# Hybrid encoder layer on eight cores: the last stage gates on unnormalised tiles, takes its reciprocal roots by Newton steps on GpSimd and transposes p first

## The reference, cut to what matters

```python
def rmsnorm(x, g):
    r = lax.rsqrt(jnp.mean(xf * xf, axis=-1, keepdims=True) + EPS)
    return (xf * r).astype(x.dtype) * g
...
        x = x + mix @ w_out[i]
        h = rmsnorm(x, g_ffn[i])
        x = x + hier_moe(h, ...)          # top-1 group, top-2 of its 8 experts
        gate = jax.nn.sigmoid(rmsnorm(x, g_ple[i]) @ w_ple_gate[i])
        x = x + (p[i] @ w_ple_proj[i]) * gate
    return rmsnorm(x, g_final)
```

## Time and profile before

| what | us |
|---|---|
| median of 3 runs | 1676.73 |
| lowest, highest of them | 1671.33, 1725.31 |
| time of the profiled execution | 1667.38 |
| its span, on core 6, the slowest | 1666.1 |
| spans of the 8 cores | 1635.5 to 1666.1 |

### The profile page before, as it was taken

The page is one execution under the profiler, slowest core; times in us unless marked ns, Lnnn a source line. Parts: engine busy times, 40 slices in busy tenths (PEclk is TensorE's granted clock), DMA queues, the critical chain, the costliest instruction groups (busy, mean ns, idle before and its releaser), DMA issues.

```text
span 1666.1 us, 22293 instructions; the slowest of 8 cores (1635.5 to 1666.1 us)
## 1 busy us (share of the span) xinstructions
PE 1117.0 (67%) x7796; PEld 704.6 (42%) x7835; DVE 572.1 (34%) x1050; ACT 474.3 (28%) x756; POOL 259.4 (16%) x285
## 2 busy tenths in 40 slices
PE   0126999999999885664645185766767657731784
PEld 0123444556656443433434174545645446520332
DVE  4452221445545434444414321111212112110476
ACT  1231111434323554322213021111212112212764
POOL 2010330000001002000000121223322223237300
PEclk9999999978768797877766597878878878875887
DMA  4749699999999999999998489789898797799813
GB/s 80 177 134 127 84 113 111 110 111 109 112 110 109 110 122 128 146 183 130 150 129 131 151 256 270 201 229 242 230 287 211 211 271 192 184 168 203 174 77 127
DMA packets 79267, 266.50 MB, mean 160 GB/s; under 512 B 17033, under 2 KB 23209, under 8 KB 69936
## 3 DMA queue, kind: packets, MB, share of 16 engines
q0 software_dynamic: 53680, 153.65, 64.7%
q1 hardware_dynamic: 25472, 111.36, 20.7%
HBM read 350.94 MB, written 113.79 MB: 279 GB/s over the span
## 4 chain that ended last, share of the span: by engine, by line
PE 45%; DMA 29%; DVE 9%; issue 9%; ACT 5%; POOL 2%; DVEq 0%; SPq 0%; another core or an unknown queue 0%; ACTq 0%; POOLq 0%
DMA arena<-h2d,arena 17%; PE ps L460 10%; PE ps L561 6%; DMA arena<-xl 6%; PE ps L1164 5%; PE ps L543 4%; DMA ohd<-arena 4%; PE ps L1145 4%; PE ps L531 4%; PE ps L1361 3%; PE ps L601 2%; PE ps L877 1%; PE ps L1124 1%; POOL arena L1312 1%; PE ps L435 1%
## 5 line engine op out<-in xcount | busy, mean ns | idle before, releaser
L547 ACT ACTIVATE arena<-ps 128x1024 bf16<-128x1024 f32 (+4 forms) x152 | 137.3, 916 | 192.6 <-PE ps L543 192.3
L1145 PE MATMUL ps<-arena 128*128 128x192 bf16 x2048 | 176.2, 247 | 1.1 <-ACT arena L1131 1.1
L1145 PEld LDWEIGHTS ps<-arena 128*128 128x128 bf16 x2048 | 171.5, 98 | 8.1 <-issue 1.3
L1164 PE MATMUL ps<-arena 128*96 128x512 bf16 x512 | 153.9, 459 | 15.2 <-DVE arena L1152 11.7
L460 PE MATMUL ps<-arena 128*128 128x512 bf16 (+1 forms) x744 | 161.2, 377 | 1.0 <-issue 0.2
L1124 PE MATMUL ps<-arena 96*128 96x96 bf16 x512 | 40.7, 245 | 159.8 <-DMA arena<-h2d,arena 159.8
L877 PE MATMUL ps<-arena 128*128 128x512 bf16 x242 | 74.9, 471 | 87.1 <-DVE arena L858 42.4
L1177 POOL DMA_INDIRECT y<-arena x64 | 60.6, 946 | 368.6 <-ACT arena L1169 289.7
L561 PE MATMUL ps<-arena 128*65 128x128 bf16 (+5 forms) x784 | 112.2, 266 | 0.8 <-ACT arena L547 0.8
L460 PEld LDWEIGHTS ps<-arena 128*128 128x128 bf16 x760 | 74.0, 99 | 88.3 <-issue 2.7
L1164 PEld LDWEIGHTS ps<-arena 128*96 128x96 bf16 x512 | 71.8, 150 | 85.8 <-issue 66.7
(11 more groups left out here) (161 smaller groups left out, 1426.1 us busy)
## 6 DMA issues: line engine op xcount, KB each, us to landing
wbf<-wexp POOLq DMA_DIRECT2D x72, 1024.0 KB, 169.2
arena<-wbf SPq DMA_DIRECT2D x72, 1024.0 KB, 16.4
arena<-wexp POOLq DMA_DIRECT2D x24, 1024.0 KB, 80.4
arena<-xl SPq DMA_DIRECT2D x40, 512.0 KB, 8.9
y<-arena SPq DMA_DIRECT2D x16, 512.0 KB, 2.7
arena<-w_in POOLq DMA_DIRECT2D x3, 1536.0 KB, 18.8
h2d<-arena SPq DMA_DIRECT2D x16, 256.0 KB, 17.2
arena<-w_out POOLq DMA_DIRECT2D x1, 2048.0 KB, 108.5
```

The source lines that it names most:

```text
L547: S.op("act", lambda e: e.activation(out=PT[pi][0:nk, :, 0:w], in_=ps[0:nk, sb:sb + 2, 0:w], func=AF.Exp, scale=0.125), reads=[b_ps[sb], b ...
L1145: self.T.op("pe", lambda e, k=k, f=f, bk=bk, wt=wt, c0=c0: e.matmul(psb(bk)[:, c0:c0 + CAP], lhsT=wt[sl][:, k, 128 * f:128 * (f + 1)], rhs ...
L1164: self.T.op("pe", lambda e, f=f, j=j, hf=hf, bk=bk: e.matmul(psb(bk)[0:HC, :], lhsT=hid[s][:, f, HC * j:HC * (j + 1)], rhs=wd_b[sl][:, f, ...
```

## The change

Nothing ahead of the tail is changed, except the layout of the tail's tiles in the memory of the expert weights.

- p is transposed for all 16 tiles in one go, ahead of the steps: 32 transposes on TensorE and 4 copies of 128x1024 on ScalarE, instead of 2 transposes and a copy of 128x256 in every step.
- A memset of the new statistics tile `ss` is recorded on POOL, behind the 32 gathers. It writes the buffers `b_ss` of all 20 indices; `p_c` and `p_f` write into them.
- `p_n` multiplies X1[t] by the gain alone. The factor is given to the sigmoids as their scale.
- `p_s(i)` takes the place of `rstd_ops`, once per step for two columns: the factor of tile i and the final one of tile i - 4. VectorE adds EPS, shifts the bits and forms the first guess; then 12 small operations on GpSimd make three Newton steps.
- The transposes of the tile alternate between PSUM banks 0 and 1. All lags shrink: `p_y` comes 5 steps behind `p_c`, not 12, so 21 steps are recorded.

```diff
-        for i in range(16 + 3):
...
+        for t in range(19):
+            if t < 16:
+                p_g(t, 0)
+            if t >= 3:
+                p_g(t - 3, 1)
+        for q in range(4):
+            for i in range(8):
+                S.op("pe", lambda e, i=i, q=q: e.transpose(
+                    out=psb16(q % 2)[:, 128 * i:128 * (i + 1)], in_=pbf[:, 4 * q + i // 2, 128 * (i % 2):128 * (i % 2 + 1)],
+                    identity=ident_b), reads=[b_pbf, b_ident], writes=[b_ps[q % 2]])
+            S.op("act", lambda e, q=q: e.copy(out=pT[:, 8 * q:8 * q + 8, :],
+                                         in_=psb16(q % 2).rearrange("p (c t) -> p c t", c=8)),
+                 reads=[b_ps[q % 2]], writes=[b_pT])
+
+        S.op("pool", lambda e: e.memset(ss, 1.0), writes=b_ss)
 
         def p_c(t):
...
+            S.op("act", lambda e: e.activation(out=junk5, in_=X1[t], func=AF.Square, scale=1.0 / 32,
+                                               accum_out=ss[:, t, 0:1]),
+                 reads=b_x1[t], writes=[b_junk5, b_ss[t]])
+
+        def p_s(i):
+            b = [b_ss[i]]
+            x, y0, u = ss[:, i, :], ry[:, i, :], ru[:, i, :]
+            S.op("dve", lambda e: e.tensor_scalar(out=x, in0=x, scalar1=EPS, scalar2=None, op0=ALU.add), reads=b, writes=b)
+            S.op("dve", lambda e: e.tensor_single_scalar(out=u.bitcast(I32), in_=x.bitcast(I32), scalar=1,
+                                                         op=ALU.arith_shift_right), reads=b, writes=b)
+            S.op("dve", lambda e: e.tensor_scalar(out=y0.bitcast(I32), in0=u.bitcast(I32), scalar1=-1.0,
+                                                  scalar2=1597463007.0, op0=ALU.mult, op1=ALU.add), reads=b, writes=b)
+            for _ in range(3):
+                S.op("pool", lambda e: e.tensor_tensor(out=u, in0=y0, in1=y0, op=ALU.mult), reads=b, writes=b)
+                S.op("pool", lambda e: e.tensor_tensor(out=u, in0=u, in1=x, op=ALU.mult), reads=b, writes=b)
+                S.op("pool", lambda e: e.tensor_scalar(out=u, in0=u, scalar1=-0.5, scalar2=1.5, op0=ALU.mult,
+                                                       op1=ALU.add), reads=b, writes=b)
+                S.op("pool", lambda e: e.tensor_tensor(out=y0, in0=y0, in1=u, op=ALU.mult), reads=b, writes=b)
 
         def p_n(t):
             s = t % 2
-            S.op("dve", lambda e: e.scalar_tensor_tensor(
-                out=xn4[s], in0=X1[t], scalar=st4[:, 2, t:t + 1], in1=gple, op0=ALU.mult, op1=ALU.mult),
-                reads=b_x1[t] + [b_st4[t], b_gple], writes=[b_xn4[s]])
+            S.op("dve", lambda e: e.tensor_tensor(out=xn4[s], in0=X1[t], in1=gple, op=ALU.mult),
+                 reads=b_x1[t] + [b_gple], writes=[b_xn4[s]])
...
         def p_a(t):
...
+                S.op("act", lambda e, hf=hf, gbk=gbk: e.activation(out=sgm[hf], in_=psb(gbk), func=AF.Sigmoid,
+                                                                   scale=ry[:, t, 0:1]),
+                     reads=[b_ps[gbk], b_ss[t]], writes=[b_sgm[hf]])
...
         def p_f(t):
...
+            S.op("act", lambda e: e.activation(out=junk5, in_=X1[t], func=AF.Square, scale=1.0 / 32,
+                                               accum_out=ss[:, t + FL, 1:2]),
+                 reads=b_x1[t], writes=[b_junk5, b_ss[t + FL]])
...
-        order = ((p_e, 6), (p_a, 7), (p_m, 6), (p_t, 5), (p_d, 7), (p_q, 6), (p_n, 4), (p_c, 0), (p_f, 8), (p_y, 12), (p_r, 8))
-        for i in range(16 + 12):
-            for f_, lag_ in order:
-                if 0 <= i - lag_ < 16:
+        order = ((p_e, 2, 16), (p_a, 3, 16), (p_m, 2, 16), (p_t, 1, 16), (p_d, 3, 16), (p_q, 2, 16), (p_n, 0, 16), (p_c, 0, 16),
+                 (p_f, 4, 16), (p_s, 0, 16 + FL), (p_y, 5, 16))
+        for i in range(16 + 5):
+            for f_, lag_, n_ in order:
+                if 0 <= i - lag_ < n_:
                     f_(i - lag_)
```

More of the change, by code:

```diff
@@ L1201, in build_nc @@
         pbf = A.alloc((16, 256), BF16)
-        pT = [A.alloc((2, 128), BF16) for _ in range(2)]
+        pT = A.alloc((32, 128), BF16)
+        yt = [A.alloc((1024,), F32)]
+        assert A.top <= W_OFF[1] + 24576
+        A.top = W_OFF[2]
+        yt += [A.alloc((1024,), F32) for _ in range(2)]
+        FL = 4
+        ss, ry, ru = [A.alloc((16 + FL, 2), F32) for _ in range(3)]
+        b_ss = [Buf("ss%d" % i) for i in range(16 + FL)]
+        junk5 = A.alloc((1024,), BF16)
         xn4 = [A.alloc((1024,), BF16) for _ in range(2)]
         hT3 = [A.alloc((8, 128), BF16) for _ in range(2)]
-        assert A.top <= W_OFF[1] + 24576
-        A.top = W_OFF[2]
-        yt = [A.alloc((1024,), F32) for _ in range(3)]
         sgm = [A.alloc((512,), F32) for _ in range(2)]
@@ L1210, in build_nc @@
         b_wpg, b_wpp, b_gple, b_pbf = Buf("wpg"), Buf("wpp"), Buf("gple"), Buf("pbf")
-        b_pT = [Buf("pT0"), Buf("pT1")]
+        b_pT = Buf("pT")
         b_yg = [Buf("yg%d" % t) for t in range(16)]
@@ L1215, in build_nc @@
         b_sgm = [Buf("sgm0"), Buf("sgm1")]
+        b_junk5 = Buf("junk5")
         b_yt = [Buf("yt%d" % i) for i in range(3)]
@@ L1315, in p_g @@
                 reads=b_y2, writes=[b_yg[t]] + b_x1[t])
-        for i in range(16 + 3):
[L1318 to L1321, removed]
-        def p_c(t):
[L1324 to L1329, removed]
+        for t in range(19):
[3 more added lines that the diff above has]
+                p_g(t - 3, 1)
@@ L1340, in p_t @@
                 S.op("pe", lambda e, k=k: e.transpose(
[L1341 to L1346, removed]
+                    out=psb16(s)[:, 128 * k:128 * (k + 1)], in_=xn4[s][:, 128 * k:128 * (k + 1)],
+                    identity=ident_b), reads=[b_xn4[s], b_ident], writes=[b_ps[s]])
         def p_e(t):
             s = t % 2
[L1350 to L1354, removed]
+            S.op("act", lambda e: e.copy(out=hT3[s], in_=psb16(s).rearrange("p (k t) -> p k t", k=8)),
+                 reads=[b_ps[s]], writes=[b_hT3[s]])
         def p_m(t):
@@ L1371, in p_q @@
                     S.op("pe", lambda e, c=c, hf=hf, pbk=pbk: e.matmul(
-                        psb(pbk), lhsT=pT[s][:, c, :], rhs=wpp_b[:, c, 512 * hf:512 * (hf + 1)],
+                        psb(pbk), lhsT=pT[:, 2 * t + c, :], rhs=wpp_b[:, c, 512 * hf:512 * (hf + 1)],
                         start=(c == 0), stop=(c == 1)),
-                        reads=[b_pT[s], b_wpp], writes=[b_ps[pbk]])
+                        reads=[b_pT, b_wpp], writes=[b_ps[pbk]])
         def p_a(t):
@@ L1379, in p_a @@
                 gbk = 2 + 2 * s + hf
-                S.op("act", lambda e, hf=hf, gbk=gbk: e.activation(out=sgm[hf], in_=psb(gbk), func=AF.Sigmoid),
-                     reads=[b_ps[gbk]], writes=[b_sgm[hf]])
+                S.op("act", lambda e, hf=hf, gbk=gbk: e.activation(out=sgm[hf], in_=psb(gbk), func=AF.Sigmoid,
+                                                                   scale=ry[:, t, 0:1]),
+                     reads=[b_ps[gbk], b_ss[t]], writes=[b_sgm[hf]])
         def p_d(t):
@@ L1404, in p_y @@
             S.op("dve", lambda e: e.scalar_tensor_tensor(
-                out=yt[s], in0=X1[t], scalar=st4[:, 5, t:t + 1], in1=gfin, op0=ALU.mult, op1=ALU.mult),
-                reads=b_x1[t] + [b_st4f[t], b_gfin], writes=[b_yt[s]])
+                out=yt[s], in0=X1[t], scalar=ry[:, t + FL, 1:2], in1=gfin, op0=ALU.mult, op1=ALU.mult),
+                reads=b_x1[t] + [b_ss[t + FL], b_gfin], writes=[b_yt[s]])
             S.dma("sp", lambda e: e.dma_start(out=y[128 * t:128 * (t + 1), :], in_=yt[s]),
                   reads=[b_yt[s]], sem="d_y%d" % s)
-        order = ((p_e, 6), (p_a, 7), (p_m, 6), (p_t, 5), (p_d, 7), (p_q, 6), (p_n, 4), (p_c, 0), (p_f, 8), (p_y, 12), (p_r, 8))
-        for i in range(16 + 12):
-            for f_, lag_ in order:
-                if 0 <= i - lag_ < 16:
+        order = ((p_e, 2, 16), (p_a, 3, 16), (p_m, 2, 16), (p_t, 1, 16), (p_d, 3, 16), (p_q, 2, 16), (p_n, 0, 16), (p_c, 0, 16),
[3 more added lines that the diff above has]
+                if 0 <= i - lag_ < n_:
                     f_(i - lag_)
```

## The result

The changed kernel is slower: 1.018 times the time before, with a 95% interval of 1.013 to 1.023. That it is slower is clear; whether by more than the 2% that a measurement of this kernel can tell from no change is not. The undisturbed runs are 1702.40 and 1704.87 us; the median of all four, 1721.67, holds two in which the cores of one die ran at a lower clock.

What follows compares the result with a forecast made beforehand. The tail was taken as bound by gathers, then TensorE's 5.30 us step plus square-root table loads. Terms +37.7 - 11.8 - 2.3 = +23.6 gave execution 1691.0 us, 1.014 of 1667.38; forecast 1696, range 1682 to 1715.

Steps and rivals of the forecast that it cites:

- start, to the first product: Tail's start: the memset behind POOL's gathers holds ScalarE and VectorE, so VectorE's first product comes 37.7 us later.
- loop, to the last product: The 15 steps from first to last tile's product: 89.4 us against 101.15, so 11.8 less, with no table loads.
- end: From the last tile's product to the span's end: 16.1 us instead of 18.4, so 2.3 less.
- I take 6.2: Full loop step: 6.2 us, between the free case and the gap case, with 5.3 and 7.8 as ends.
- rival A: Loop: VectorE and POOL exclude each other, full step 7.5 us, `p_y` waits over 1 us; slower by 2.4%; chance 0.24.
- the gap case: Full loop step: one POOL operation gets into each of four gaps between VectorE's operations, giving 6.4 us instead of 7.8.
- The price of 0.35 per Newton operation: Newton chain on POOL: 12 dependent operations at 0.35 us each, 4.2 us per step.
- My VectorE sum of 5.6: Full loop step: VectorE needs 4.8 us plus 0.8 for three more small operations, 5.6, above TensorE's 5.30.
- Newton 4.2 with nothing to hide it: Tail's end, after the last tile's sums: the Newton chain adds 4.2 us, part of an end of 16.1.
- C (not held): Start: ScalarE isn't held and steps run beside the gathers; execution 1631 us, 2.2% faster; chance 0.04.
- B (Newton free): Loop: Newton operations at 0.27 us, well overlapped, full steps of 5.4; execution 1682.2 us; chance 0.20.
- was never on the path: Each step's 128x256 copy of p on ScalarE: removing it saves nothing, as ScalarE idled 0.76 us per step.

Runs made afterwards that it cites:

- e5_v4_hold: `v4_quads` with the memset of `ss` back on POOL behind the gathers; tail 189.9 us, against 138.4 for `v4_quads`.
- v4_quads: Changed kernel with roots on VectorE by four tiles, two Newton steps, longer lags, memset ahead of the gathers; tail 138.4 us, 0.976 of the time before.
- e2_two_newton: Changed kernel with two Newton steps instead of three, 8 GpSimd operations instead of 12; tail 186.9 us, against 204.6.
- e8_wide_memsets: Changed kernel with the Newton steps replaced by 12 GpSimd memsets of 128x128, which read nothing; tail 187.7 us, against 204.6.
- e7_early_p: The kernel before with only the transposes of p moved ahead of the steps; tail 171.1 us, against 174.1.
- e6_memsets: Changed kernel with the Newton steps replaced by 12 GpSimd memsets of 128x2, which read nothing; tail 184.8 us, against 204.6.

## Why the prediction was right, and where it was off

The forecast was the likeliest case: slower by 1.4%, within the bound of 2%. Measured: 1.8%, with an interval that reaches past 2%. The range held the undisturbed runs. The tail grew by 28.5 us between the two slowest cores, whose rows the document shows (30.5 between the means), where the sum said 23.6. Term by term:

| term | said | measured, slowest cores | measured, mean of 8 cores |
|---|---|---|---|
| start, to the first product | +37.7 | +32.9 (55.3 to 88.2) | +34.5 |
| loop, to the last product | -11.8 | -7.6 (101.15 to 93.5) | -7.3 |
| end | -2.3 | +3.2 (18.4 to 21.6) | +3.2 |

The mechanism of the start, the largest term, was right. That the sum came within 5 us is in part luck: the start was put 4.8 too large, while the loop's gain was put 4.2 too large and the end 5.5 too small, so the first miss took back half of the other two.

*The start* is shown: by the wait of 75.4 us for the memset, and by `e5_v4_hold`, which has no other difference from `v4_quads`. The size was 4.8 too large. I had put two table loads on the path, 2.6 us; the only one now is made for the first copy of p, at 1493.79, in idle time, and the sigmoid needs none. The second copy came 6.98 us behind the first, not 8.13: the first group of matmuls took 5.20 instead of over 5.97. The granted clock stood at 0.50, its level of 1.2 GHz, from the group's start at 1578.4 to 1581.5, and was 0.95 on average in the next 2 us; before, it stood at 0.50 from 1536.6 to 1540.5 and was 0.73 in the next 2.5. The memset shows 0.70, not 0.2, but it begins inside the last gather's span, and ScalarE starts 0.24 behind that span's end, about as worked out.

*The loop*: the roots' 21.6 us went; no load is left, and where GpSimd doesn't bound, 15 steps take 79.4 (`e2_two_newton`) and 79.1 (`e8_wide_memsets`), not 101.15. "I take 6.2" was 6.43, of the same cause that the earlier trace rows hinted at and rival A described; the gap case, one operation let through at each end of VectorE's, had said 6.4 and is what the timeline shows. The price of 0.35 per Newton operation was measured as 0.34. My VectorE sum of 5.6 was 5.45: what follows `p_n` starts 1.14 behind it instead of 1.20, and what follows the last small operation 0.17 instead of 0.27. TensorE's 5.30 came back only in the first two steps. The 4.1 us by which the loop was longer than said are 2.5 in 11 full steps at 6.43 for 6.2, 1.0 more in the first of them, which took 7.48 because `p_y` waited 2.02 for GpSimd, and 0.7 in the last two, 5.63 each for 5.3.

*The end* is the step that failed in sign: "Newton 4.2 with nothing to hide it". There are two chains, for tiles 14 and 15, on one engine, each stretched to 5.0 by the one operation beside `p_y`; the second starts when the first is through, and the first only when tile 13's is, 4.3 us behind the last product's start. `e8_wide_memsets` shows 18.7 there (1680.62 to 1699.3) against 21.6.

Of the rivals, C (not held) and B (Newton free) are out. A had the right mechanism and too high a price: not all of GpSimd's work is shut out, only the four operations that meet VectorE's two-input ones. Its sign, `p_y` waiting over 1 us for GpSimd in each step, was missed by little, at 0.98.

*The early transposes of p*: their copy "was never on the path" holds for the undisturbed steps. At the pairs of table loads it was on it, for 1.2 us in all (`e7_early_p`).

## What to carry to other kernels

An operation recorded on a queue behind a series of gathers is held until the last is issued, and so is every engine that waits for it; in `e5_v4_hold` a memset of 48 values a row cost 51 us this way. Before moving small work onto an idle engine, read what stands ahead of it in that queue, and which operations of its neighbour shut it out. A chain of tiny dependent operations is cheaper by groups of tiles: 9 operations per four tiles on VectorE replaced 15 per tile.

## What was not expected of the hardware

A GpSimd operation that is held up gets through at the end of each of VectorE's two-input operations, even when the next follows at once: the 0.62 and 0.44 beside the two sums. The record of VectorE's own operation does not grow by it (1.28 for `p_y` both before and after). GpSimd's memset of 128x40 shows 0.70 and begins inside the last gather's span, that of 128x2 shows 0.10 (`e6_memsets`) and that of 128x128 0.205 (`e8_wide_memsets`); why the first is so long wasn't tried.
